# Halves of normalized rows transposed in two steps, and high products first, in a two-block transformer kernel

## The reference

```python
# first block, for l in 0, 1
proj = x @ w_in[l]                       # 1024 -> 8200: retention q,k,v,g; mLSTM qk,v,o,i,f; two merge gates
mix  = (sigmoid(g_a) * (o_ret @ w_proj_ret[l]) + sigmoid(g_b) * (o_ml @ w_proj_mlstm[l])) @ w_out[l]
x = layer_norm(ALPHA * x + mix, ln1_g[l], ln1_b[l])
gu = x @ w_gate_up[l];  hidden = silu(gu[:, :2816]) * gu[:, 2816:]
x = layer_norm(ALPHA * x + hidden @ w_down[l], ln2_g[l], ln2_b[l])
# second block, for l in 0, 1
hn = rms_norm(h, norm_gain[l]);  proj = hn @ w_in_2[l]       # 1024 -> 3584
h = h + concat(dilated attention, RG-LRU, stick-breaking attention) @ w_out_2[l]
# end
out = rms_norm(h, final_gain)
```

## Time and profile before

| | us |
|---|---|
| median of 3 runs | 1164.36 (1163.63 to 1165.45) |
| the profiled execution | 1165.11 |
| its span, first to last instruction | 1163.3 |
| PE busy | 1150.4 (99%) |
| DVE busy | 772.8 (66%) |
| ACT busy | 576.0 (50%) |
| granted TensorE clock | 0.999 of full speed |

### The profile page before, as it was taken

How to read it: one execution, slowest core, us unless ns; L and a number is a source line. 1 busy time by engine, 2 the same in 40 slices (tenths; PEclk the granted TensorE clock), 3 DMA queues, 4 the chain that set the end, 5 groups by cost and what they waited for, 6 DMA issues and landing times.

```text
span 1163.3 us, 18514 instructions
## 1 busy us (share of the span) xinstructions
PE 1150.4 (99%) x7762; PEld 1045.8 (90%) x7762; DVE 772.8 (66%) x1051; ACT 576.0 (50%) x663; POOL 28.8 (2%) x36
## 2 busy tenths in 40 slices
PE   9999999999999999999999999999999999999997
PEld 7989998998999988899998898899988789978996
DVE  4887856667655556697774667755555667785676
ACT  5565455442544434555544534444443456755663
POOL 0000000001000000000000000000000100010000
PEclk9999999999999999999999999999999999999999
DMA  9654454556665464655455456665656453447320
GB/s 330 235 199 159 152 199 163 190 183 197 227 216 184 163 205 139 225 174 170 135 186 198 163 199 217 203 210 184 199 191 204 157 206 122 144 136 253 121 98 37
DMA packets 129874, 211.62 MB, mean 182 GB/s; under 512 B 6528, under 2 KB 52608, under 8 KB 129664
## 3 DMA queue, kind: packets, MB, share of 16 engines
q1 hardware_dynamic: 128048, 204.15, 52.4%
q0 software_dynamic: 1744, 6.29, 1.8%
HBM read 209.37 MB, written 1.05 MB: 181 GB/s over the span
## 4 chain that ended last, share of the span: by engine, by line
PE 89%; ACT 3%; DVE 3%; DMA 2%; issue 2%; SPq 0%; POOL 0%; POOLq 0%; DVEq 0%; ACTq 0%
PE ps L500 87%; DMA raw<-in_w_in 2%; ACT wh L986 1%; DVE wl L1417 1%; PE ps L727 1%; PE ps L633 1%; PE ps L827 0%; ACT L1025 0%; POOL small L455 0%; ACT L1028 0%; DVE xl L1511 0%; SPq L436 0%; ACT ee L1304 0%; PE ps L809 0%; DVE zz L1981 0%
## 5 line engine op out<-in xcount | busy, mean ns | idle before, releaser
L1417 DVE TENSOR_TENSOR wl<-raw,wh 128x2048 fp32r<-128x2048 f32 (+1 forms) x185 | 414.8, 2248 | 170.4 <-ACT wh L986 170.1
L986 ACT ACTIVATE wh<-raw 128x2048 fp32r<-128x2048 f32 (+1 forms) x189 | 358.2, 1900 | 189.3 <-PE ps L500 165.1
L500 PE MATMUL ps<-xh,wh 128*128 128x256 f32 x1328 | 371.3, 280 | 1.2 <-issue 1.2
L500 PE MATMUL ps<-xl,wh 128*128 128x256 f32 x1328 | 368.1, 278 | 0.0
L500 PE MATMUL ps<-xh,wl 128*128 128x256 f32 x1312 | 364.3, 278 | 0.0
L500 PEld LDWEIGHTS ps<-xh,wh 128*128 128x128 f32 x1328 | 250.2, 188 | 4.3 <-issue 3.7
L500 PEld LDWEIGHTS ps<-xl,wh 128*128 128x128 f32 x1328 | 250.1, 188 | 0.2
L500 PEld LDWEIGHTS ps<-xh,wl 128*128 128x128 f32 x1312 | 246.6, 188 | 0.0
L500 PE MATMUL ps<-wh,xh 128*128 128x512 f32 (+1 forms) x440 | 172.1, 391 | 3.2 <-DVE wl L1417 1.7
L500 PE MATMUL ps<-wh,xl 128*128 128x512 f32 (+1 forms) x440 | 168.5, 383 | 0.0
L500 PE MATMUL ps<-wl,xh 128*128 128x512 f32 (+1 forms) x440 | 168.4, 383 | 0.0
(11 more groups left out here) (303 smaller groups left out, 1476.4 us busy)
## 6 DMA issues: line engine op xcount, KB each, us to landing
raw<-in_w_in SPq DMA_DIRECT2D x90, 1024.0 KB, 5.0
raw<-in_w_gate_up SPq DMA_DIRECT2D x88, 512.0 KB, 5.0
raw<-in_w_down SPq DMA_DIRECT2D x20, 1024.0 KB, 5.0
raw<-in_w_out SPq DMA_DIRECT2D x16, 1024.0 KB, 4.8
raw<-in_w_proj_ret SPq DMA_DIRECT2D x8, 1024.0 KB, 4.8
raw<-in_w_proj_mlstm SPq DMA_DIRECT2D x8, 1024.0 KB, 5.0
rows<-in_ln_g POOLq DMA_DIRECT2D x4, 512.0 KB, 4.5
rows<-in_ln_b POOLq DMA_DIRECT2D x4, 512.0 KB, 6.1
```

The costliest lines, as they stand in the source:

```text
L500: return pe.matmul(o, a, b, start=start, stop=False, skip_group_check=True)
L986: act.activation(stretch(wh, u, 0, m), source(u)[:, 0:m], ACT.Copy).then_inc(s_hi, 1)
L1417: dve.tensor_tensor(stretch(wl, u, a, nk * n), source(u)[:, a:nk * n], f32(stretch(wh, u, a, nk * n)), ALU.subtract).then_inc(s_lo, 1 if a ...
```

## The change

`half_k` calls `mid` twice: `mid(0)` ahead of row block `mid_at`, `mid(1)` behind the unit's last row block. `turn_x` takes a tuple `halves`, so that each call transposes one q. For the t = 0 turns in `by_half`, and the t = 1 turn of the second block's `pair`, q = 0 goes at `mid_at` and q = 1 at the unit's end; for the pairs of the first block both still go together at row block 2 (`None if q else turn_x(...)`). For dn1 of layer 1, `mid_at` goes from 2 to 3. In `pair`, unit[0] gets a `version`: row blocks 0 and 1 do their high-part products (`xh` with `wh` and `wl`) after a wait for `s_xh` alone, and the two `xl` products follow behind the wait for `xl`.

```diff
--- before.py
+++ after.py
@@ -578,19 +578,31 @@
                             slot += 1
                 side(plan, steps, l, name, slot)
 
-            def half_k(t, bank, lh, ll, ready, k, unit, last, mid=None, mid_at=2):
+            def half_k(t, bank, lh, ll, ready, k, unit, last, mid=None, mid_at=3, version=None):
                 u, nk, h_, l_ = unit
                 for kk in range(nk):
                     if mid and kk == mid_at:
-                        mid()
+                        mid(0)
                     if t == 0 and kk in (0, nk // 2):
                         pe.wait_ge(s_lo, 2 * u + 1 + (kk > 0))
+                    if version is not None and kk < 2:
+                        if kk == 0:
+                            pe.wait_ge(s_xh, 4 * version + 2 * t + 1)
+                        mm(bank[:, :], lh[:, kk, tok_half(t)], h_[:, kk, :], kk == 0)
+                        mm(bank[:, :], lh[:, kk, tok_half(t)], l_[:, kk, :], False)
+                        if kk == 1:
+                            ready(0, t)
+                            for j in range(2):
+                                mm(bank[:, :], ll[:, j, tok_half(t)], h_[:, j, :], False)
+                        continue
                     ready(k + kk, t)
                     r = tok3(bank[:, :], lh, ll, k + kk, t, h_[:, kk, :], l_[:, kk, :], k + kk == 0)
                 if t == 1:
                     r.then_inc(s_used, 1)
                 elif last:
                     r.then_inc(s_half, 1)
+                if mid:
+                    mid(1)
 
             def by_half(name, l, head, tail, lh, ll, ready, mid, mid_at=3):
                 k = 0
@@ -609,11 +621,12 @@
                         half_k(t, bank, lh, ll, ready, kt, unit, end, mid if t == 1 and end else None, mid_at)
                         kt += unit[1]
 
-            def pair(a, b, l, ready, after, third, fifth, at=2):
+            def pair(a, b, l, version, after, third, fifth, at=2):
+                ready = x_part(version)
                 unit = [take() for _ in range(3)]
                 for t in range(2):
                     bank = open_bank(a, l, t)
-                    half_k(t, bank, xh, xl, ready, 0, unit[0], False)
+                    half_k(t, bank, xh, xl, ready, 0, unit[0], False, version=version)
                     half_k(t, bank, xh, xl, ready, KU, unit[1], True)
                     if t == 1:
                         third()
@@ -624,8 +637,8 @@
                     if t == 0:
                         fifth()
 
-            def turn_x(l, tag, t, v, src, seen):
-                for q in range(2):
+            def turn_x(l, tag, t, v, src, seen, halves=(0, 1)):
+                for q in halves:
                     name = f"{tag}{t}{q}"
                     bank, fill = open_aux(name, l)
                     pe.wait_ge(seen, v + 2 * t + q + 1)
@@ -774,7 +787,7 @@
                     one("mv0", xh, xl, xw, "tok", 5)
                     one("mv1", xh, xl, xw, "tok")
                 else:
-                    pair("mv0", "mv1", l, x_part(2), lambda: turn_x(0, "xb", 1, 4, X[:, 1, :], s_xn), nothing, nothing)
+                    pair("mv0", "mv1", l, 2, lambda q: None if q else turn_x(0, "xb", 1, 4, X[:, 1, :], s_xn), nothing, nothing)
                 gate(l)
                 one("mqk0", xh, xl, xw, "col")
                 one("mqk1", xh, xl, xw, "col")
@@ -789,16 +802,16 @@
                 one("ym0", omh, oml, gated_ready("om", l), "col")
                 one("ym1", omh, oml, gated_ready("om", l), "col")
                 one("out0", mxh, mxl, mix_ready(l), "tok")
-                by_half("out1", l, 0, 2, mxh, mxl, mix_ready(l), lambda: turn_x(l, "xa", 0, 8 * l, X[:, 0, :], s_xn))
-                pair("ff0", "ff1", l, x_part(2 * l + 1), lambda: turn_x(l, "xa", 1, 8 * l, X[:, 1, :], s_xn),
+                by_half("out1", l, 0, 2, mxh, mxl, mix_ready(l), lambda q: turn_x(l, "xa", 0, 8 * l, X[:, 0, :], s_xn, (q,)))
+                pair("ff0", "ff1", l, 2 * l + 1, lambda q: None if q else turn_x(l, "xa", 1, 8 * l, X[:, 1, :], s_xn),
                      lambda: hidden_turn(l, 0, 0), lambda: hidden_turn(l, 0, 1))
                 for j in range(2, 11):
                     one(f"ff{j}", xh, xl, x_whole(2 * l + 1), "col")
                 one("dn0", hdh, hdl, hidden_ready(l), "tok", 6)
                 if l == 0:
-                    by_half("dn1", l, 4, 2, hdh, hdl, hidden_ready(l), lambda: turn_x(0, "xb", 0, 4, X[:, 0, :], s_xn), 3)
+                    by_half("dn1", l, 4, 2, hdh, hdl, hidden_ready(l), lambda q: turn_x(0, "xb", 0, 4, X[:, 0, :], s_xn, (q,)), 3)
                 else:
-                    by_half("dn1", l, 3, 3, hdh, hdl, hidden_ready(l), lambda: turn_x(1, "xb", 0, 0, xn(0), s_rm), 2)
+                    by_half("dn1", l, 3, 3, hdh, hdl, hidden_ready(l), lambda q: turn_x(1, "xb", 0, 0, xn(0), s_rm, (q,)), 3)
 
             def rope_turn(l, c):
                 for t in range(2):
@@ -953,7 +966,7 @@
             for l in range(DEPTH):
                 tag, at = ("xb", 1) if l == 0 else ("2x", 0)
                 one = lambda name, mode: group(SIDE2, steps2, name, l, 2, xh, xl, x_whole(4 + l), mode)
-                pair("q", "k", l, x_part(4 + l), lambda: turn_x(at, tag, 1, 4 * l, xn(1), s_rm), nothing, nothing, 3 - l)
+                pair("q", "k", l, 4 + l, lambda q: turn_x(at, tag, 1, 4 * l, xn(1), s_rm, (q,)), nothing, nothing, 3 - l)
                 one("av", "tok")
                 one("ag", "col")
                 one("cqk", "col")
```

## The result

The changed kernel took 1167.6 us (median of 17 runs, 1163.57 to 1170.73), the kernel before 1164.05 (17 runs, 1163.41 to 1165.45): ratio 1.002, 95% interval 1.0013 to 1.0027 (that is the ratio of the averages, 1166.85 to 1164.27; the medians stand at 1.003, since the runs lie in groups). The forecast was 1164.8 and no change; the median lies 1.0 us above the upper end of the range, and the interval is clear of 1. The profiled execution took 1168.65 us, with a span of 1166.9 where before had 1163.3: 3.6 us.

What follows compares the result with a forecast made beforehand. TensorE, busy in 99% of the span, was taken as the bound. Terms +0.30, +0.12, −0.20 and +0.17 summed to +0.39 us, taking the median from 1164.36 to 1164.8 us; range 1162.5 to 1166.6.

Steps and rivals of the forecast that it cites:

- The first stall: First turn of layer 0: PE's next product waits 0.60 us for DVE's first `xl` copy; the change removes this.
- the lag: DVE's chain behind the split turn runs 0.57 us late, with 0.42 to spare before PE needs the third unit's `wl`.
- (a): Turns out1 to ff0, layers 0 and 1: 0.60 us won, given back plus 0.15 more each; +0.30 us for both.
- (b): Turn dn1 to mv0 at layer 0's end: late second half of `wl`, +0.12 us, or +0.02 by the short release.
- the release: Time from the end of a DVE result until PE goes on: 0.15 us taken, bounds 0.15 and 0.05.
- (c): Turn dn1 to q at layer 1's end: DVE 0.44 us late, then the split gains; net −0.20 us.
- (d): Pair q, k of layer 1: 0.08 us of `wl` wait plus one switch of 0.09; +0.17 us, bounds 0 and +0.25.
- a switch would be free: Skill-based alternative for an added transpose-to-product switch: no cost, against 0.09 us taken; the sum would be 0.30.
- The step that failed: Whole kernel: no product, transpose or copy added, copies keep their sizes; behind the out1 to ff0 turns, no further cost.
- Rival 1: Late DVE chain is covered, so PE does not wait behind the second turn: −2.35 us, 1162.0; chance 9%.
- Rival 2: DVE's lag is about double, some 1.1 us instead of 0.57, at four turns: +2.6 us, 1167.0; chance 5%.
- Rival 3: First stall is not lifted because something other than `xl` held the first product: +0.6 us, 1165.0; chance 6%.

Runs made afterwards that it cites:

- e9: Against the kernel with only the new product order (halves transposed together): second half of the third unit's `wl` written twice; 1166.32 us.
- e12: Against the kernel with only the new product order: just 448 columns of the third unit's second-half `wl` written twice; 1164.05 us.
- e10: Against the kernel with only the two-step transposes (old product order): second half of the third unit's `wl` written twice; 1169.66 us.
- third-transpose kernel: Against the changed kernel: the last transpose ahead of the long ff2 to ff10 stretch written twice, once a layer; 1167.57 us, 3.11 above before.

## Why the prediction was right and wrong

- **The first stall and the lag (a), (b): right**, in place and kind. The stall of 0.60 went (0.68 in fact: the split's transposes came closer together), DVE's lag was 0.55 for 0.57, the wait for the third unit's `wl` took its place. The mis-sized term is the release: PE followed DVE by 0.05, not 0.15, the lower of my two bounds. I had taken 0.15 as the row nearest in kind, and it was a wait for `xl`; the other row, at 919.02, was a wait for this very kind of copy. In the traces each wait for `wl` at these turns ends 0.05 behind the copy, and each for `xl` or `sg` 0.15, whether transposes or products stand ahead. So these terms were +0.06 for +0.42.
- **dn1 to q (c): right**, −0.27 for −0.20. **The last pair (d):** +0.1 for +0.17; the switch of 0.09 is in the rows (0.31 between the first two products), the `wl` wait was 0.05. From the Trainium skill's pull-ahead of weights ("TensorE: Matmul & The Clock Gate", "Step-by-step: what each phase is for") I had worked out that a switch would be free; here it is not.
- **The step that failed** is the one from "No product, transpose or copy is added" to "Nothing" for what stands behind the turns: it put no price on products that stay the same. The same products took 4.4 ns more each, over 815 of them: 3.59 us in the traced execution, and by the clusters of the times such a stretch stands in some two thirds of the executions. The trace of before held both pitches (118.0 in the 287 products behind om, 113.5 in ff2 to ff10), and I had not looked at it for the price of a product by stretch.
- **Rival 1** was a real prize, though not of this change: with the lag gone (order alone), T falls by 0.52 three times; my 0.42 had the long release in it. **Rival 2's** sign came true by another mechanism; the lag was not double. **Rival 3** is out.
- The turns alone would have given 1164.0 to 1164.1 for the shown 1164.05; the executions without a slow stretch (1163.6 to 1165.3) agree with that.

**What stays open** is what draws the pitch. By the clusters, the stretch of ff2 to ff10 was slow in the kernels that have the split, the new order and PE's idle 0.42 together (41 runs, 28 with at least one slow stretch), and in none of the 92 others of this study with one or two of these. Before itself is less clear: two of its runs beside the experiments, 1167.89 and 1167.29, lie 3.0 and 2.8 above the medians of their sets (1164.85 and 1164.47), and neither was traced; they may be the same thing. So it is not shown that the slow pitch needs the change, only that it is far more frequent with it (28 of 41 runs against 2 of before's 111). e9 and e12 have the order and a wait, without the split, e10 the split and a wait, and none shows it, but their idle times are 0.58 to 1.18 long, not 0.42. Whether the split itself or the exact length counts was not settled.

The traces say where it is not decided: at the stretch itself. In the executions traced as slow, the 24 products just ahead of it, between the last two `hidden_turn`s (two transposes each), are already different, and the other way round. Over the same 20 distances of starts they take 2.35 us in before (117.8 ns each) and 2.27 in the changed kernel (113.5):

```profile
303.85 0.28 PE L500 MATMUL ps<-xh,wh 128*128 128x256 f32 x1
...
306.20 0.28 PE L500 MATMUL ps<-xh,wl 128*128 128x256 f32 x1
```

```profile
303.91 0.28 PE L500 MATMUL ps<-xh,wh 128*128 128x256 f32 x1
...
306.18 0.28 PE L500 MATMUL ps<-xh,wl 128*128 128x256 f32 x1
```

Behind the two transposes each takes the other's pitch. The slow layer 1 of the third-transpose kernel does the same, behind three. A difference stands still earlier, behind the first `hidden_turn`: 9.48 us after the restart in both slow cases, 9.45 or 9.46 in the four fast ones of these kernels (284.87 to 294.35; in the other execution of the same program 283.90 to 293.35). But before has 9.43 and 9.46, so that being late by itself does not mark it. These are the rows of the changed kernel, and then of its other execution:

```profile
294.35 0.39 PE L500 MATMUL ps<-wl,xh 128*128 128x512 f32 x1
```

```profile
283.90 0.50 PE L500 MATMUL ps<-wh,xh 128*128 128x512 f32 x1 [0.41 <-DVE wl L1430]
...
293.35 0.39 PE L500 MATMUL ps<-wl,xh 128*128 128x512 f32 x1
```

## What to carry to other kernels

Before splitting a step that feeds two engines in order, follow each engine's queue to the next place where the bound engine meets it: the slack there (0.57, less the 0.05 of the release: 0.52 here), not the stall removed, is what a delay may cost. Of two edits for one stall take the one that moves nothing on the other engines; the product order alone was worth 2.4 us (1.9 in the trace), and the split undid it wherever a `wl` stood behind it. And compare the time per product stretch by stretch, not only the waits: a PE that is 100% busy can be 4% slower.

## What the hardware showed unexpectedly

In this program a run of loads and products with 256 columns has two stable pitches, 113.3 and 117.8 ns (113.5 and 117.9 with the first products), at the same granted clock (1.00, its 2.4 GHz level) and with the same operands. It settles on one within about six products, and the longest stretch kept it for 90 us. Where the pitch changed, two to five transposes or a few products of 128 columns stood between. One repeated transpose made the 287 products behind om fast in both layers, two made 147 others slow, and one did nothing to these. With 512 columns an undisturbed run stood at 226.7 ns in every trace. The Trainium skill ("TensorE: Matmul & The Clock Gate", "Back-to-back issue gap") gives one gap for an isolated matmul, N / 2.4 + 2.5, by which an estimate for 256 columns is 109 ns, and says that in a stream of loads and matmuls both set the spacing; neither of the two pitches of these traces is 109.
